# Retention values as split products, a reordered beginning, a last pass in two column parts, and an earlier bias addition

## The reference

```python
def retention_mixer(x, w_in, norm_g, w_out):
    q, k, v, g = split_cols(x @ w_in, RET_SPLITS)          # 1024, 1024, 2048, 2048 columns
    q = rotary(q.reshape(bsz, l, RET_HEADS, RET_DK))       # 4 heads of 256
    k = rotary(k.reshape(bsz, l, RET_HEADS, RET_DK)) * RET_DK ** -0.5
    v = v.reshape(bsz, l, RET_HEADS, RET_DV)               # 4 heads of 512
    o = head_group_norm(retention_chunked(q, k, v), norm_g)
    return (o.reshape(bsz, l, RET_VAL) * jax.nn.silu(g)) @ w_out
# retention: o_t = sum over s <= t of (q_t . k_s) * decay_head ** (t - s) * v_s
h = layer_norm(DN_ALPHA * h + 0.5 * swiglu_2(h, ffn_w_in[i, 1], ffn_w_out[i, 1]), ln_g[i, 2], ln_b[i, 2])
```

## Time and profile before

| | |
|---|---|
| runs | 1626.92 us median (1626.63 to 1627.74) |
| profiled execution | 1628.09 us, its span 1626.3 us |
| TensorE busy | 1615.2 us (99%), granted clock 0.999 |
| VectorE busy | 950.0 us (58%) |
| ScalarE busy | 773.4 us (48%) |
| GpSimd busy | 79.4 us (5%) |
| HBM | 304.59 MB read, 188 GB/s over the span |

### The profile page before, as it was taken

The page is one execution under the profiler, slowest core; times in us unless marked ns, Lnnn a source line. Parts: engine busy times, 40 slices in busy tenths (PEclk is TensorE's granted clock), DMA queues, the critical chain, the costliest instruction groups (busy, mean ns, idle before and its releaser), DMA issues.

```text
span 1626.3 us, 18392 instructions
## 1 busy us (share of the span) xinstructions
PE 1615.2 (99%) x7774; PEld 1341.4 (82%) x7774; DVE 950.0 (58%) x942; ACT 773.4 (48%) x810; POOL 79.4 (5%) x102
## 2 busy tenths in 40 slices
PE   9999999999999999999999999999999999999998
PEld 6888897788888888888988888888888997888886
DVE  6555466676544685455668545665445557585553
ACT  7444446655443774442656434354443435454340
POOL 0121000000000000001010000000000141000000
PEclk9999999999999999999999999999999999999999
DMA  9756574466554776453647646666565554576560
GB/s 300 223 178 208 169 240 141 155 206 214 182 173 164 248 223 188 156 208 113 233 156 249 190 156 207 205 199 188 163 204 184 198 179 139 181 234 190 160 217 26
DMA packets 222017, 306.84 MB, mean 189 GB/s; under 512 B 8816, under 2 KB 144112, under 8 KB 221808
## 3 DMA queue, kind: packets, MB, share of 16 engines
q1 hardware_dynamic: 216944, 290.02, 54.6%
q0 software_dynamic: 4416, 15.05, 3.0%
q10 hardware_dynamic: 576, 0.59, 0.1%
HBM read 304.59 MB, written 1.05 MB: 188 GB/s over the span
## 4 chain that ended last, share of the span: by engine, by line
PE 97%; DVE 1%; ACT 1%; issue 0%; DMA 0%; ACTq 0%; DVEq 0%
PE bank L651 29%; PE bank L662 28%; PE bank L655 25%; PE bank L615 3%; PE bank L666 3%; PE bank L693 2%; PE bank L695 2%; PE bank L696 2%; DVE low L1516 0%; DMA h<-in_x 0%; ACT hiw L1152 0%; PE bank L1035 0%; PE bank L1115 0%; PE bank L844 0%; PE bank L825 0%
## 5 line engine op out<-in xcount | busy, mean ns | idle before, releaser
L1516 DVE TENSOR_TENSOR low<-raw,hiw 128x2048 fp32r<-128x2048 f32 (+1 forms) x295 | 631.8, 2151 | 390.5 <-ACT hiw L1152 390.2
L1152 ACT ACTIVATE hiw<-raw 128x2048 fp32r<-128x2048 f32 (+1 forms) x280 | 522.0, 1871 | 367.8 <-DMA raw<-in_ffn_w_out 88.1
L651 PE MATMUL bank<-hiw,xh 128*128 128x512 f32 x1404 | 385.0, 396 | 0.2 <-ACT xh L1157 0.2
L662 PE MATMUL bank<-low,xh 128*128 128x512 f32 x1404 | 376.1, 390 | 0.0
L655 PE MATMUL bank<-hiw,xl 128*128 128x512 f32 x1232 | 330.2, 390 | 0.0
L662 PEld LDWEIGHTS bank<-low,xh 128*128 128x128 f32 x1404 | 263.5, 188 | 55.7 <-DVE low L1516 0.2
L651 PEld LDWEIGHTS bank<-hiw,xh 128*128 128x128 f32 x1404 | 257.2, 188 | 53.0 <-issue 2.5
L655 PEld LDWEIGHTS bank<-hiw,xl 128*128 128x128 f32 x1232 | 231.3, 188 | 49.5
L651 PE MATMUL bank<-hiw,th 128*128 128x512 f32 x528 | 144.8, 392 | 0.0
L655 PE MATMUL bank<-hiw,tl 128*128 128x512 f32 x528 | 143.3, 389 | 0.0
L662 PE MATMUL bank<-low,th 128*128 128x512 f32 x528 | 143.2, 389 | 0.0
(11 more groups left out here) (256 smaller groups left out, 1163.4 us busy)
## 6 DMA issues: line engine op xcount, KB each, us to landing
raw<-in_ffn_w_in SPq DMA_DIRECT2D x176, 512.0 KB, 4.9
raw<-in_ffn_w_out SPq DMA_DIRECT2D x40, 1024.0 KB, 5.0
raw<-in_ret_w_in SPq DMA_DIRECT2D x24, 1024.0 KB, 5.1
raw<-in_ffn_w_gate SPq DMA_DIRECT2D x43, 512.0 KB, 4.4
raw<-in_ffn_w_up SPq DMA_DIRECT2D x43, 512.0 KB, 5.5
raw<-in_ffn_w_down SPq DMA_DIRECT2D x20, 1024.0 KB, 5.0
raw<-in_w_in SPq DMA_DIRECT2D x16, 1024.0 KB, 5.7
raw<-in_gla_w_in SPq DMA_DIRECT2D x12, 1024.0 KB, 5.2
```

The costliest lines, as they stand in the source:

```text
L651: pe.matmul(o[:, :], tokens(0, k), whi[:, k, :], start=start and k == 0, stop=False, skip_group_check=True)
L662: ins = pe.matmul(o[:, :], tokens(0, k), wlo[:, k, :], start=False, stop=end, skip_group_check=True)
L1152: act.activation(hiw[s][:, 0:n], raw[s][:, 0:n], ACT.Copy).then_inc(hi.mark(i), 1)
L1516: dve.tensor_tensor(low[s][:, c0:c1], raw[s][:, c0:c1], hiw[s][:, c0:c1].bitcast(F32), ALU.subtract).then_inc(lo.mark(*what), 1)
```

## The change

The values and masked scores of retention become split operands (`rvh`, `rvl`, `rsh`, `rsl`), and their product becomes three float32r products for each float32 one. In the beginning the first column half of both token halves is loaded, transposed and split before the second column half; `g0T` is loaded from GpSimd's queue; the dummies are 8, 4 and 3; `pe_first` takes the high products ahead of the low ones. The last pass is made in two parts of 256 columns, the second in bank 0 (`LAST`), with an order of its own for VectorE behind it. In attention VectorE's bias addition and maximum of unit 1 stand ahead of a weight tile's low part. Memory: `rvl0` lies on `xn`, `rvl1` behind `rg0`, `rsp` and `rsl` behind `rgn`, on places of weight slots 5 and 6 that are closed then.

```diff
+        LAST = bank[0]
@@ sp_program
-            for j in range(2):
-                sp.dma_start(half(h[:, 1, :], j), half(A["x"][0, P:2 * P, :], j)).then_inc(x_in[1][j].mark(j), 16)
+            for t in range(2):
+                sp.dma_start(half(h[:, t, :], 1), half(A["x"][0, t * P:(t + 1) * P, :], 1)).then_inc(
+                    x_in[t][1].mark(1), 16)
...
+            for t, c, n, what in ((0, 0, 512, 0), (0, 512, 512, 1), (1, 0, 512, 0), (1, 512, 256, 2), (1, 768, 256, 3)):
+                sp.wait_ge(vec.sem, vec.of("h", "out", t, what))
+                sp.dma_start(out[0, t * P:(t + 1) * P, c:c + n], h[:, t, c:c + n]).then_inc(out_in.mark(t, c), 16)
@@ pool_program
+            pool.dma_start(g0T[:, :], A["g0T"]).then_inc(gain_0.mark(0), 16)
             pool_gain(pool, 1)
@@ pe_first
+            pe.wait_ge(turn_hi.sem, turn_hi.of("x", "f1", 0, 0))
+            for K in ((0, 1), (2, 3)):
+                pe_hi(pe, 0, *(() if K[0] else ("first",)))
+                for k in K:
+                    pe.matmul(o[:, :], S[0][:, k, 0:P], whi[:, k, :], start=k == 0, stop=False, skip_group_check=True)
+                if K[0] == 0:
+                    pe.wait_ge(turn_lo.sem, turn_lo.of("x", "f1", 0, 0))
+                for k in K:
+                    pe.matmul(o[:, :], S[1][:, k, 0:P], whi[:, k, :], start=False, stop=False, skip_group_check=True)
+                pe_lo(pe, 0, *(() if K[0] else ("first",)))
+                for k in K:
+                    ins = pe.matmul(o[:, :], S[0][:, k, 0:P], wlo[:, k, :], start=False, stop=False,
+                                    skip_group_check=True)
+                if K[0] == 0:
+                    pe_turn_in(pe, 0, 1)
             ins.then_inc(passed.mark(0, 0), 1)
+
+        def pe_last(pe, i, S, k0):
+            whi, wlo = weight(i)
+            for c, o in ((0, ACC[1][1]), (1, LAST)):
+                for m, w in ((0, whi), (1, whi), (0, wlo)):
+                    for k in range(4):
+                        ins = pe.matmul(o[:, 0:256], S[m][:, k0 + k, P:2 * P], w[:, k, c * 256:(c + 1) * 256],
+                                        start=c == 1 and m + k == 0 and w is whi, stop=w is wlo and k == 3,
+                                        skip_group_check=True)
+                ins.then_inc(passed.mark(i, 1) if c else passed.mark(i, 1, "first"), 1)
@@ pe_ffn
+                        if (j, n, t) == (0, 0, 1):
+                            pe_turn_in(pe, 1, 1)
@@ pe_ret: values
-                            pe.wait_ge(fn.sem, fn.of("rv", n - 2, t))
+                            pe.wait_ge(vec.sem, vec.of("rvl", n - 2, t))
...
-                pe.wait_ge(vec.sem, vec.of("rs", hd))
+                pe.wait_ge(vec.sem, vec.of("rsl", hd))
...
+                    for s in range(t + 1):
+                        q = slice(t * P, t * P + P) if s == 0 else slice(256, 384)
+                        pe.matmul(b[:, :], rsh[:, hd, q], rvh[:, s, c], start=s == 0, stop=False, skip_group_check=True)
+                        pe.matmul(b[:, :], rsh[:, hd, q], rvl[s][:, c], start=False, stop=False, skip_group_check=True)
+                        ins = pe.matmul(b[:, :], rsl[:, hd, q], rvh[:, s, c], start=False, stop=s == t,
                                         skip_group_check=True)
@@ pe_program
-            pe_turn_in(pe, 0)
-            pe_idle(pe, 10)
+            pe_turn_in(pe, 0, 0)
+            pe_idle(pe, 4)
+            pe_turn_in(pe, 1, 0)
+            pe_idle(pe, 3)
@@ act_ret
+            def scores_high(hd):
+                act.wait_ge(vec.sem, vec.of("rs", hd))
+                act.activation(rsh[:, hd, :], rsp[:, hd, :], ACT.Copy).then_inc(fn.mark("rsh", hd), 1)
+
+            scores_high(0)
...
                 if n < 3:
+                    scores_high(n + 1)
                     norms(n)
@@ act_program (g0T's DMA left out here, x of both token halves, first columns, in its place)
-            act_turn_in(act, 0, 1)
             act_high(act, 0)
             act_turn_in(act, 1, 0)
+            act_turn_in(act, 0, 1)
+            act_high(act, 1)
             act_turn_in(act, 1, 1)
             act_high(act, 2)
@@ dve_last (called for the last edge, second token half)
+            for j in range(2):
+                dve.wait_ge(passed.sem, passed.of(e.final[2], 1) if j == 0 else passed.of(e.final[3], 1, "first"))
+                dve.scalar_tensor_tensor(half(hh, j), ACC[1][j][:, :], s, half(hh, j), ALU.mult, ALU.add).then_inc(
+                    vec.mark("s", "out", 1, j), 1)
+                dve.wait_ge(vec.sem, vec.of("s", "out", 1, j))
+                statistics(2 * j)
+                if j == 0:
+                    statistics(1)
+            dve.wait_ge(passed.sem, passed.of(e.final[3], 1))
+            dve.scalar_tensor_tensor(hh[:, 768:1024], LAST[:, 0:256], s, hh[:, 768:1024], ALU.mult, ALU.add).then_inc(
+                vec.mark("s", "out", 1, 2), 1)
+            dve.wait_ge(vec.sem, vec.of("s", "out", 1, 2))
+            statistics(3)
...
@@ dve_mixer (scores(u) is cut into sums(u), to the maximum, and shares(u))
-            scores(0)
+            sums(0)
+            shares(0)
             for u in range(8):
+                if u == 0:
+                    sums(1)
                 dve_lows(dve, ahead(at["mg"][u]))
                 if u == 0:
-                    scores(1)
+                    shares(1)
...
                 if u < 6:
-                    scores(u + 2)
+                    sums(u + 2)
+                    shares(u + 2)
@@ dve_ret
+            def unit(n, t):
+                c = slice(n * 512, n * 512 + 512)
+                dve.wait_ge(fn.sem, fn.of("rv", n, t))
+                dve.tensor_tensor(rvl[t][:, c], PAIRS[n % 2][t][:, :], rvh[:, t, c].bitcast(F32), ALU.subtract).then_inc(
+                    vec.mark("rvl", n, t), 1)
...
+            def scores_low(hd):
+                dve.wait_ge(fn.sem, fn.of("rsh", hd))
+                dve.tensor_tensor(rsl[:, hd, :], rsp[:, hd, :], rsh[:, hd, :].bitcast(F32), ALU.subtract).then_inc(
+                    vec.mark("rsl", hd), 1)
...
                 dve_lows(dve, ahead(at["rg"][2 * n + 1]))
+                if n == 0:
+                    scores_low(0)
                 if n < 3:
                     scores(n + 1)
                     norms(n)
+                    scores_low(n + 1)
```

More of the change, by code:

```diff
@@ L246, in build @@
         h = sb("h", [P, 2, D])
+        with ExitStack() as ar:
+            rvl0 = sb("rvl0", [P, 2048], F32R, ar)
         xn = sb("xn", [P, 2, D])
@@ L624, in pe_turn_x, with pe_turn_in @@
                 pe_turn(pe, ("x", nx, t, g), quads(half(x_source(nx, t), g)))
[L626 to L629, removed]
+        def pe_turn_in(pe, t, g):
+            pe.wait_ge(x_in[t][g].sem, x_in[t][g].of(g))
+            pe_turn(pe, ("x", "f1", t, g), quads(half(h[:, t, :], g)))
         def pe_hi(pe, i, *part):
@@ L739, in pe_ffn @@
                     for t in range(2):
-                        if j + n + t == 0:
-                            pe.wait_ge(turn_lo.sem, turn_lo.of("x", name, 0, 0))
-                        elif j == 0:
+                        if j == 0 and n + t:
                             pe.wait_ge(turn_hi.sem, turn_hi.of("x", name, t, n))
@@ L771, in pe_ffn @@
                         pe.wait_ge(turn_lo.sem, turn_lo.of("t", name, 2 * g))
-                    pe_pass(pe, dn[8 + n], T, groups[g][0], t, ACC[t][n % 2], False, g == 5)
+                    if (t, n) == (1, 3) and f.nx == "out":
+                        pe_last(pe, dn[11], T, groups[g][0])
+                    else:
+                        pe_pass(pe, dn[8 + n], T, groups[g][0], t, ACC[t][n % 2], False, g == 5)
         def pe_project(pe):
@@ L1479, in act_program @@
         def act_program(act):
-            for j in range(2):
-                act.dma_start(half(h[:, 0, :], j), half(A["x"][0, 0:P, :], j)).then_inc(x_in[0][j].mark(j), 16)
-                if j == 0:
+            for t in range(2):
+                act.dma_start(half(h[:, t, :], 0), half(A["x"][0, t * P:(t + 1) * P, :], 0)).then_inc(
+                    x_in[t][0].mark(0), 16)
+                if t == 0:
                     act.dma_start(ident[:, :], A["c_ident"]).then_inc(const_in.mark("ident"), 16)
-            act.dma_start(g0T[:, :], A["g0T"]).then_inc(gain_0.mark(0), 16)
             act.wait_ge(vec.sem, vec.of("eps"))
@@ L1620, in dve_first @@
         def dve_first(dve, e, t):
+            if e.nx == "out" and t:
+                dve_last(dve, e)
+                return
             if e.kind == "ln":
@@ L1755, in scores, with shares @@
                 dve.tensor_reduce(nm, p2, AX, ALU.max, negate=True).then_inc(vec.mark("max", u), 1)
+            def shares(u):
+                nm, sm, rs_ = [st[:, 64 + 6 * u + 2 * m:66 + 6 * u + 2 * m] for m in range(3)]
                 dve.wait_ge(fn.sem, fn.of("exp", u, 1))
@@ L1901, in dve_ret @@
         def dve_ret(dve):
-            dve_lead(dve, "ret", at["rv"][0:4])
```

(8 more changed lines are left out.)

69 lines of the change are left out of this document (39 added, 30 removed).

## The result

The changed kernel takes 1623.45 us in the median (1621.76 to 1623.83, 13 runs), the kernel before 1627.72 (1626.63 to 1627.99, 13 runs beside it). The ratio is 0.9974, 95% interval 0.9965 to 0.9982: faster by 4.3 us. The forecast was 1622.8 and 4.1 off the time before; rival 4 (1620.8) and rival 1 (1624.1) lie on either side.

A forecast was written before the change was run, and what follows sets the result against it. TensorE, busy 1615.2 us of a 1626.3 us span, was taken as the bound. Retention values -2.1, attention -0.6, beginning -1.3 and end -0.1 sum to -4.1: median 1626.92 becomes 1622.8 us, range 1620.7 to 1624.9.

The forecast's parts named there:

- rival 4: Whole kernel: all of it pays, with an early clock and a beginning chain that does not bind; 1620.8 us, chance 0.09.
- rival 1: Beginning of the kernel: it gives nothing; 1624.1 us, chance 0.18.
- Values: Retention values: nine float32r products replace three float32 ones, 2.04 us a head instead of 2.57; -2.1 us for four heads.
- The spare times: Retention: low scores ready 2.1 us early at head 0, 2.4 at heads 1 to 3; first bank 0.4 early behind head 3.
- Rival 2: Retention: norms run late, TensorE waits at every head's values and behind head 3, the 2.1 is gone; 1624.9 us, chance 0.10.
- rival 3: Retention values: the nine products run at the float32 pace, 7.7 us a head instead of 2.57; 1645.4 us, chance 0.03.
- Attention: Scores behind attention's first transposes: moving VectorE's bias addition ahead of the weight residue removes TensorE's wait; -0.6 us, ends -0.7 and 0.
- End: Last pass in two column parts and the finish behind it: +0.15, -0.5, +0.25, sum -0.1 us; ends -0.6 and +0.5.
- Beginning: Start to the first gated transposes: they come at 33.4 or 35.1 instead of 35.62; middle -1.3 us, ends -2.9 and +0.9.
- The chain that I put behind tile 0's pass over the second tokens: Beginning: ScalarE's and VectorE's work up to the gated product ends 3.5 + 13.9 us behind that pass, at 33.4 or 35.1.
- ScalarE's first copy at 7.3 released by TensorE: Beginning, sign of being right: ScalarE's first copy comes at 7.3 instead of 8.69, released by TensorE and not by a DMA.
- a first copy still waiting for g0T: Beginning, sign of being wrong: ScalarE's first copy still waits for g0T, which was expected issued at 0.5 and landed at 5.3.

The follow-up runs named there:

- the first execution: First profiled execution of the changed kernel, the fastest of its 13 runs: 1621.76 us, gated transposes at 32.09.
- the second execution: Second profiled execution of the changed kernel, no edit, the slowest of six further runs: 1623.57 us, gated transposes at 33.95.

## Why the prediction was right

**Values.** 9 x 0.227 = 2.04 a head and -2.1 in all: measured 2.04, -2.07 in the trace, -2.1 in the medians of retention alone. The float32 price of 0.857 and the float32r price of 0.227 for the same width were the whole sum. The spare times were right to 0.3 us. The rule that the prediction set beside them, a drain at each table load (the Trainium skill, "ScalarE: Activation LUTs", "What ACT_TABLE_LOAD costs"), isn't seen: the load begins 0.01 behind the copy and the root 0.02 behind the load. Rival 2 (a wait at every head) fell, since TensorE waits at none, and rival 3 (the float32 pace, 0.857) fell with the spacing of 0.227.

**Attention.** -0.6 forecast, -0.65 by undoing it, -0.56 between the first two traces.

**End.** -0.1 forecast, -0.26 measured, with the right parts: from the start of the last pass to VectorE 2.92 before (1616.26 to 1619.18) and 3.06 after, +0.14 (forecast +0.15); from there to the root 1.70 and 1.22, -0.48 (forecast -0.5); the finish 2.93 and 3.19, +0.26 (forecast +0.25); from VectorE's end to the span's 2.49 and 2.31, -0.18, which the forecast left at "a little less" and nothing.

**Beginning.** -1.3 forecast. Against medians it gave 1.6 alone, and within the whole 4.5 (1627.6 to 1623.1) less 3.0 (2.07, 0.65, 0.26), 1.5. (1627.6 lies between the medians of before beside the two sets of runs, 1623.1 is the median of all 19 runs.) The profiled pair has -3.5, beyond the end of -2.9 that I had set. Four points:
- The chain that I put behind tile 0's pass over the second tokens was exact. Its length was 3.5 + 13.9 = 17.4 from the pass's end to the end of the gated product. Measured: 14.66 to 32.03 in one execution, 16.52 to 33.90 in the other, 17.37 and 17.38.
- Its start was what I had too late: 16.0 at the earliest, and it was 14.66. I let the first product start at 10.5 or later, from the transposes at 6.17 of before. In the first execution the identity released TensorE at 5.15, the clock was up at about 4.0, behind seven dummies 0.43 apart, and the first product came at 8.19. In the second, with the identity at 6.12 as I had assumed, the clock rose at about 10.2 and not at 12.7, and the first product came at 10.38. I had taken the landings and the clock's rise from one trace as if they were fixed.
- "ScalarE's first copy at 7.3 released by TensorE" came true in the second execution (7.33, behind 3.57 of idle for TensorE's transposes) and not in the first, where it was at 5.96 and g0T was still the releaser: issued at 1.26, not 0.5, and landed 4.7 later, as the mask's 4.8 let expect. By the prediction's own sign ("a first copy still waiting for g0T") it was wrong there; the wait cost little, since the transposes that the copy needs had ended only at 5.8.
- That -1.3 came out near 1.6 is in part luck. I took the middle between transposes at 33.4 and at 35.1; the two executions had 32.09 and 33.95, each over 1.1 earlier. But the 35.62 that I subtracted from was late itself: 1628.09 stands 0.5 above the median of its kernel. The one error took back part of the other.

So rival 1 (the beginning gives nothing) fell. Rival 4 wanted an early clock and a chain that doesn't bind: the first execution had the early clock, but the chain bound in both, by the 0.47 at the gated transposes.

## What to carry to other kernels

Price a matmul by the spacing of its starts: a float32 product of 512 columns cost 0.857 us here and its three float32r parts 0.68, so splitting paid as soon as the extra roundings had idle time to lie in. Where a kernel's beginning depends on landings and on the clock, one profiled execution is a draw: compare two kernels by the start times behind the beginning, and profile the same kernel twice before believing a difference of a microsecond or two. An engine that prepares weights ahead should not have tiles that are wanted later in front of the operation that the busiest engine waits for; that the wait went is seen in the traces, while the gain is hardly seen in the times.

## What the hardware showed that I had not expected

The identity, 64 KB behind 256 KB of x on ScalarE's queue, released the first transposes between 5.06 and 5.30 in five profiled executions of kernels with the new beginning, and between 6.05 and 6.44 in four others; in the tenth the twelve dummies ended behind its landing. It landed 3.8 to 4.0 us behind its issue in six of the ten and 4.8 to 5.2 in four.

Without the dummy products between the transposes the median was 0.9 to 1.3 us higher, although TensorE has nothing else to do there.

The clock can fall again at the start. With retention alone changed the first transposes, at 6.01, came 0.11 us apart (2.4 GHz) and the dummies from 7.87 came 0.43 apart (1.2 GHz) until about 11.3, and the profile grants 0.54 from 7.6 to 10.9. TensorE had stood idle for 1.31 us ahead of 6.01 and for 0.71 ahead of 7.38. But ahead of the first rise the granted clock says 1.00 in every trace here, also where dummies 512 wide come every 0.43 us: there the spacing is the measure.
